# Two feed-forward layers whose output product is done in a second phase, as seven block products over eleven pairs

## The reference, cut to what matters

```python
def swiglu(x, w_in, w_out):
    gate, up = jnp.split(x @ w_in, 2, axis=-1)
    return (jax.nn.silu(gate) * up) @ w_out
...
        h = layer_norm(DEEPNORM_ALPHA * h + m, ln_mix_g[layer], ln_mix_b[layer])
        f = swiglu(h, ffn_w_in[layer], ffn_w_out[layer])
        h = layer_norm(DEEPNORM_ALPHA * h + f, ln_ffn_g[layer], ln_ffn_b[layer])
```

## Time and profile before

| what | value |
|---|---|
| median of three runs | 2750.70 us (2750.08 to 2753.43) |
| profiled execution, span from first to last instruction | 2747.0 us |
| the same execution's granted clock, mean share of full speed | 0.968 |
| matmuls of PE in it | 13124 |

### The profile page before, as it was taken

One profiled execution on the slowest core, in us unless ns is written; L12 is line 12 of the kernel. 1 busy time (PEld: TensorE's weight loads), 2 busy tenths in 40 slices (PEclk: granted clock), 3 DMA queues, 4 the chain that ended last, 5 costly groups with the idle time before them and its releaser, 6 DMA issues. The chain is left out here.

```text
span 2747.0 us, 40526 instructions
## 1 busy us (share of the span) xinstructions
PE 2554.0 (93%) x13124; PEld 2139.3 (78%) x13124; DVE 1835.2 (67%) x3179; ACT 818.5 (30%) x1382; POOL 830.4 (30%) x600
## 2 busy tenths in 40 slices
PE   6787699999999999978999999997899999999996
PEld 5676577878888888866888888886787888888885
DVE  8879527776666666583667666667577666666666
ACT  3223323332332232213222233222134223322321
POOL 2968320333332332411111111110024333323332
PEclk8889899999999999998999999998899999999998
DMA  4333214134443443412010110100404344434431
GB/s 138 91 100 108 81 39 153 43 105 140 126 122 107 133 119 108 145 54 69 24 39 23 38 31 23 38 23 16 153 28 119 110 140 125 122 107 134 118 117 75
DMA packets 388063, 246.16 MB, mean 90 GB/s; under 512 B 23936, under 2 KB 370176, under 8 KB 387072
## 3 DMA queue, kind: packets, MB, share of 16 engines
q1 hardware_dynamic: 387968, 244.92, 29.9%
HBM read 227.10 MB, written 17.76 MB: 89 GB/s over the span
## 5 line engine op out<-in xcount | busy, mean ns | idle before, releaser
L968 DVE TENSOR_TENSOR h<-h,ps 128x512 f32<-128x512 f32 x320 | 218.9, 685 | 154.8 <-PE ps L542 154.4
L2209 POOL TENSOR_TENSOR w_lo<-w_raw_plain,w_hi 128x1024 fp32r<-128x1024 f32 x38 | 91.8, 2423 | 556.2 <-ACT w_hi L62 556.2
L2237 PE MATMUL ps<-aT_hi,w_hi 128*128 128x512 f32 x624 | 251.6, 403 | 3.7 <-DVE hg_q_raw L2498 1.9
L2237 PE MATMUL ps<-aT_hi,w_lo 128*128 128x512 f32 x624 | 246.2, 394 | 0.0
L2237 PE MATMUL ps<-aT_lo,w_hi 128*128 128x512 f32 x624 | 244.7, 392 | 0.0
L1086 POOL TENSOR_TENSOR s5o_w_sets_plain<-s5o_w_sets_plain 128x512 f32<-128x512 f32 x100 | 138.0, 1385 | 220.4 <-DMA s5o_w_sets_plain<-in_ffn_w_in_dram 220.4
L1086 POOL TENSOR_TENSOR hgo_w_sets_plain<-hgo_w_sets_plain 128x512 f32<-128x512 f32 x100 | 137.2, 1376 | 221.6 <-DMA hgo_w_sets_plain<-in_ffn_w_in_dram 221.6
L484 PE MATMUL ps<-aT_hi,hgo_w_sets 128*128 128x512 f32 x640 | 203.1, 393 | 1.1 <-DVE hgo_w_sets L912 1.1
L484 PE MATMUL ps<-aT_hi,s5o_w_sets 128*128 128x512 f32 x640 | 203.0, 393 | 1.1 <-DVE s5o_w_sets L912 1.1
L542 PE MATMUL ps<-s5o_w_hi,s5o_hid_hi 128*128 128x512 f32 x352 | 138.2, 393 | 14.1 <-DVE aT_lo L905 13.5
L62 ACT ACTIVATE s5o_w_sets<-s5o_w_sets_plain 128x512 fp32r<-128x512 f32 x152 | 92.7, 627 | 177.3 <-POOL s5o_w_sets_plain L1086 151.2
(11 more groups left out here) (394 smaller groups left out, 6344.3 us busy)
## 6 DMA issues: line engine op xcount, KB each, us to landing
s5o_w_sets_plain<-in_ffn_w_in_dram SPq DMA_DIRECT2D x208, 256.0 KB, 3.3
hgo_w_sets_plain<-in_ffn_w_in_dram SPq DMA_DIRECT2D x208, 256.0 KB, 3.3
w_raw_plain<-in_hg_w_in_dram SPq DMA_DIRECT2D x40, 512.0 KB, 4.1
s5o_w_sets_plain<-in_ffn_w_in_dram SPq DMA_DIRECT2D x96, 128.0 KB, 2.6
hgo_w_sets_plain<-in_ffn_w_in_dram SPq DMA_DIRECT2D x96, 128.0 KB, 2.7
s5o_w_lo_plain<-in_ffn_w_out_dram SPq DMA_DIRECT2D x11, 1024.0 KB, 5.0
hgo_w_lo_plain<-in_ffn_w_out_dram SPq DMA_DIRECT2D x11, 1024.0 KB, 5.0
h<-in_x_dram SPq DMA_DIRECT2D x4, 1024.0 KB, 8.9
```

Source lines behind the costliest of these rows:

```text
L968: v.tensor_tensor(to, to, ps[:, 4 + m % 4, :], ALU.add).then_inc(S["out_acc"], 1)
L2209: g.tensor_tensor(w_lo[b][:, :, :], w_raw[b][:, :, :], w_hi[b][:, :, :].bitcast(F32), ALU.subtract).then_inc(E[f"w_lo_done{b}"], 1)
L2237: ins = t.matmul(ps[:, half, :], w[b][:, kk, :], x[:, kk, cols], start=(kk == 0 and q == 0), stop=(kk == KT - 1 and q == 2))
```

## The change: what it does

- The output product is taken out of the loop. The loop only makes hidden tiles, two per iteration, and its two tiles use banks 0 to 3 and 4 to 7 in turn (`4 * second + to`). PE goes from position 13 straight to position 0 of the next iteration.
- The hidden pair and four sums or differences of it (`hidden_sum`, four operations on POOL for each pair) are stored to a DRAM scratch, seven 128x512 blocks for each of the 11 pairs, by SP.
- A second phase of 7 x 11 = 77 steps follows (`out_step`): for each of the seven products `OUT_PRODUCTS`, eleven pairs are accumulated in four PSUM banks (the other four for the next product). A step is 4 token tiles x 3 = 12 matmuls. Its operands are one stored block and one or two blocks of w_out, loaded by `load_pair`; DVE subtracts where there are two (`pair_sum`), ACT makes hi (`pair_hi`, 1024 columns), DVE lo (`pair_lo`). Eleven places form a ring; a place is reloaded when the step that used it is done, and at most six loads run ahead of `pair_hi`.
- DVE adds a finished product to h once for each product (`accumulate(p)`), placed six steps into the next one. In the last product the first two pairs go as before and the last nine go tile by tile (`last_tile`). The first layer now also normalises tiles 0 to 5 by way of ACT and POOL (`rescale`, `add_bias`).
- The order of ACT's and DVE's instructions in a tile is new (`tile`; `ahead(n)` is the split of the set n positions behind the first of the tile, which may belong to the next iteration). `SLOTS` and `SLOT_AT` are as before.

Of the code, cut to its core:

```diff
         return ("11", 0, "21-11") if tt < PAIRS else ("22", 1, "12-22")
...
+    OUT_PRODUCTS = ["11*11", "S1*T1", "S2*T2", "S4*22", "S3*T3", "12*21", "22*T4"]
+    A_PART = [0, 3, 5, 6, 4, 1, 2]
+    B_PARTS = [((0, 0),), ((0, 0), (0, 1)), ((1, 1),), ((1, 1),), ((0, 1), (1, 1)), ((1, 0),), ((1, 0),)]
+    B_SUM = [False, True, True, False, True, False, True]
...
+    LAST_STEPS = STEPS - NG
...
+    plain_homes = [k.plain[f"{tag}_home{n}"] for n in range(4)]
...
+    RING = [("home", 3), ("block", 3), ("block", 4), ("slot", 0), ("slot", 1), ("slot", 2),
+            ("hi", 0), ("hi", 1), ("hi", 2), ("hi", 3), ("lo", 3)]
+    LAST_RING = RING[6:8] + RING[0:6] + [("home", 0), ("home", 1), ("home", 2)]
+    EARLY_RING = 3
...
+            def store_early(j, of):
+                s.dma_start(scratch_part(j, 0, 1), first_half(of)).then_inc(S["early_stored"], 16)
+            def store_late(j):
+                s.wait_ge(S["hidden_sum"], 4 * j + 4)
+                carry(s, j)
+                s.dma_start(scratch_part(j, 1, 2), late_hidden).then_inc(S["late_stored"], 16)
+                s.dma_start(scratch_part(j, 3, 4), plain_homes[1][:, :]).then_inc(S["late_stored"], 16)
             def load_rows(gamma, beta):
...
+                final = isinstance(i, int) and i == LAST - 1
+                for pos in range(SLOTS, 10):
+                    load_set(i, pos)
                 if not (isinstance(i, int) and i == 0):
-                    load_w2(i)
-                for pos in range(SLOTS, 2 * NP):
+                    store_late(i - 1)
+                for pos in range(10, 2 * NP):
                     load_set(i, pos)
-                if not (isinstance(i, int) and i == LAST - 1):
+                s.wait_ge(S["merged"], (2 * i + 1) * NMERGE)
+                carry(s, i)
+                store_early(i, early_hidden)
+                if not final:
                     for pos in range(SLOTS):
                         load_set(i + 1, pos)
...
+            def load_pair(n):
+                p, j = n // NG, n % NG
+                before = used_before(n)
+                if before is not None:
+                    s.wait_ge(S["step"], before + 1)
+                if n >= IN_SEMS:
+                    s.wait_ge(S["pair_hi"], n - IN_SEMS + 1)
+                (_, plain), sem = pair_of(n)[1], S[f"set_in{n % IN_SEMS}"]
+                s.dma_start(first_half(plain), scratch_part(j, A_PART[p], 1)).then_inc(sem, 16)
+                tiles = (2 * j + 1, 2 * j + 2) if j < LAST else (0, NF_LAST)
+                for m, (q, dh) in enumerate(B_PARTS[p]):
+                    to = plain if m == len(B_PARTS[p]) - 1 else pair_of(n)[1][0]
+                    s.dma_start(second_half(to), w_out_v[:, tiles[q], dh * HALF:(dh + 1) * HALF]).then_inc(sem, 16)
...
+            s.wait_ge(S["late_stored"], 32 * LAST)
+            s.wait_ge(S["plain_hi"], 2 * len(PLAIN_SETS))
+            for n in range(EARLY_RING):
+                load_pair(n)
+            s.wait_ge(S["part"], 16)
+            for n in range(EARLY_RING, LAST):
+                load_pair(n)
+            store_late(LAST)
+            s.wait_ge(S["late_stored"], 32 * NG)
+            for n in range(LAST, LAST_STEPS):
+                load_pair(n)
+            s.wait_ge(S["out_acc"], accs_before(5))
             for to, of in first_weights:
...
                         t.wait_ge(S["kept"], 3 * (f - 1) + r - 3)
                         if r > 4:
                             t.wait_ge(S["merged"], (f - 1) * NMERGE + r - 4)
-                    elif not (isinstance(f, int) and f == 1):
-                        t.wait_ge(S["merged"], (f - 2) * NMERGE + (6, 7, 9, 8)[r])
+                    elif not (isinstance(f, int) and f <= 2):
+                        t.wait_ge(S["merged"], (f - 3) * NMERGE + (6, 7, 9, 8)[r])
+                    elif f == 2:
+                        pass
                     elif r == 0:
...
-            def outputs(i, tiles, hidden):
...
-                    for q in range(FG):
-                        for n, (x, w) in enumerate(((hid_hi, w2_hi), (hid_hi, w2_lo), (hid_lo, w2_hi))):
-                            ins = t.matmul(ps[:, 4 + m % 4, :], x[:, q, tt * P:(tt + 1) * P],
-                                           w[:, q, dh * HALF:(dh + 1) * HALF],
...
+            def pair_product(n, tt):
+                p, j = n // NG, n % NG
+                (a_hi, a_lo), (b_hi, b_lo) = operands(n)
+                rows = slice(tt * P, (tt + 1) * P)
+                for m, (x, w) in enumerate(((a_hi, b_hi), (a_hi, b_lo), (a_lo, b_hi))):
+                    ins = t.matmul(ps[:, out_bank(p, tt), :], x[:, rows], w, start=(j == 0 and m == 0),
+                                   stop=(j == LAST and m == 2))
+                return ins
+            def out_step(n):
+                p, j = n // NG, n % NG
+                t.wait_ge(S["pair_lo"], n + 1)
+                if n == 0:
+                    t.wait_ge(S["merged"], (NF_LAST - 1) * NMERGE)
+                if n == NG:
+                    t.wait_ge(S["half_product"], 4)
+                if p >= 2 and j == 0:
+                    t.wait_ge(S["out_acc"], accs_before(p - 1))
+                if p == 2 and j == 0:
+                    t.wait_ge(S["first_copied"], PAIRS)
+                for tt in range(PAIRS):
+                    ins = pair_product(n, tt)
+                ins.then_inc(S["step"], 1)
+            def last_tile(tt):
+                for n in range(LAST_STEPS + EARLY_STEPS, STEPS):
+                    t.wait_ge(S["pair_lo"], n + 1)
+                    ins = pair_product(n, tt)
+                ins.then_inc(S["last_tile"], 1)
             for n, (dh, kh) in enumerate(PIECES):
...
-            def keep(f, n):
+            def keep(f, n, second):
                 a.wait_ge(S["product"], (f - 1) * NP + n + 1)
                 carry(a, f)
                 if n == 2:
                     a.wait_ge(S["merged"], (f - 1) * NMERGE + 4)
                     carry(a, f)
+                elif isinstance(f, int) and f == 1:
+                    a.wait_ge(S["half_product"], n + 1)
                 else:
-                    a.wait_ge(S["hid"], 2 * f)
+                    a.wait_ge(S["merged"], (f - 2) * NMERGE + (10 if n else 8))
                     carry(a, f)
-                a.activation(act_out[0 if n == 0 else 1][:, :], ps[:, n, :], ACT.Copy).then_inc(S["kept"], 1)
+                a.activation(act_out[0 if n == 0 else 1][:, :], ps[:, 4 * second + n, :], ACT.Copy).then_inc(S["kept"], 1)
...
+            def pair_hi(n):
+                p, j = n // NG, n % NG
+                (hi, _), (_, plain) = pair_of(n)
+                a.wait_ge(S[f"set_in{n % IN_SEMS}"], parts_in(n))
+                if B_SUM[p]:
+                    a.wait_ge(S["pair_sum"], sums_to(n))
+                    if p in (1, 2):
+                        a.activation(difference(j), second_half(plain), ACT.Copy)
+                split_hi(a, hi, plain).then_inc(S["pair_hi"], 1)
...
+            def tile(i, second):
+                f, final = 2 * i + 1 + second, isinstance(i, int) and i == LAST - 1
+                def ahead(n):
+                    pos = NP * second + n
+                    if pos < 2 * NP:
+                        set_hi(i, pos)
+                    elif not final:
+                        set_hi(i + 1, pos - 2 * NP)
+                ahead(4)
+                keep(f, 0, second)
+                ahead(5)
+                keep(f, 1, second)
+                ahead(6)
+                ahead(7)
+                keep(f, 2, second)
+                ahead(8)
+                silu_late(f)
+                ahead(9)
+                silu_early(f)
+                ahead(10)
...
+            def merge(f, step, second, to_hidden):
...
+                    10: (second_half(to_hidden), late, diff[:, :], ALU.mult)}[step]
                 v.tensor_tensor(to, one, other, op).then_inc(S["merged"], 1)
...
+            def pair_sum(n):
+                p, j = n // NG, n % NG
+                if B_SUM[p]:
+                    hi, lo = (second_half(a) for a in pair_of(n)[1])
+                    v.wait_ge(S[f"set_in{n % IN_SEMS}"], parts_in(n))
+                    if p == 2:
+                        v.wait_ge(S["pair_hi"], NG + j + 1)
+                    elif p == 6:
+                        v.wait_ge(S["pair_hi"], 2 * NG + j + 1)
+                    v.tensor_tensor(lo, lo, hi if len(B_PARTS[p]) == 2 else difference(j), ALU.subtract
+                                    ).then_inc(S["pair_sum"], 1)
+            def pair_lo(n):
+                v.wait_ge(S["pair_hi"], n + 1)
+                (hi, lo), (_, plain) = pair_of(n)
+                v.tensor_tensor(lo, plain, hi.bitcast(F32), ALU.subtract).then_inc(S["pair_lo"], 1)
...
+                ahead(4)
+                ahead(5)
+                merge_steps(1, 2)
+                ahead(6)
+                merge_steps(3, 4)
+                ahead(7)
+                merge_steps(5, 6)
+                ahead(8)
```

(25 more changed lines are left out.)

494 lines of the change are left out of this document (250 added, 244 removed).

## The result

The changed kernel takes **3023.05 us** in the median (3019.72 to 3025.55, 4 runs) where the kernel before takes 2750.56 (2750.08 to 2753.43): a ratio of 1.0984, 95% interval 1.0968 to 1.1001. Forecast were 2990 us, in a range from 2915 to 3060. The sign, the range and the mechanism are right; the forecast is 33 us short. One term, the clock, is short by 52 us over the 18 seams; other terms of the seam were too high and hide part of that. Of all executions behind the numbers of this document one was slow (6365.38 us at a granted clock of 0.421, in e12); it counts in no ratio, and only in that run's median.

A forecast was written before the change was run, and what follows sets the result against it. PE was taken to bound the kernel, busy 93% of the span and never stopping in the loop. Terms -60.2 + 293 + 12 - 5 = +240 on 2747.0 gave 2987 profiled, 2990 us median, range 2915 to 3060.

The forecast's parts named there:

- matmuls removed: Output product falls from 1056 to 924 matmuls a layer, at 0.228 us each: -60.2 us for both layers.
- seam, first wait: Passing between loop iterations, position 13 waits for ACT's third copy, behind the hi of next iteration's set 0: 7.3 us.
- seam, second wait: Next iteration's set 1 loads only after position 13; its 7.6 us chain, less 2.73 hidden by position 0: 4.9 us.
- seam, third wait: Position 6 waits for a third copy delayed by POOL's hidden sums among the sums for sets 5 to 7: 2.2 us.
- seam, clock: PE runs at half clock after the 7.3 us wait, nothing taken for the 4.9 us wait: 1.9 us a seam.
- into the second phase, both layers: Entering the second phase, first lo, plain sets 4 and 5 and first pair come late: +12 us, from 4 to 24.
- the 77 steps: Second-phase steps need 2.73 us of PE each, with ACT, DVE and loads keeping ahead: no extra time.
- last product and tail: First tile of the last product about 9 us late, against old waits gone and a shorter tail: together -5 us.
- Rival B: Only slot reuse holds, not ACT's order: position 0 starts 4.8 us late in each seam, 2784 us; chance 0.06.
- rival C: Clock falls at both waits of a seam and returns late, 4 us more a seam: 3062 us; chance 0.13.
- Rival D: Second phase bound by its loads at the loop's 130 GB/s, 100 us a layer: up to 3190 us; chance 0.05.
- What would show it: Predicted trace signs: loop PE busy some 70%, position 0 every 54.5 us, named waits, half clock once per seam.

The follow-up runs named there:

- e12: On e9, PE runs the third tile of the last product ahead of the transposes of tiles 0 and 1; 2712.0 us, ratio 0.9859.
- e4: Changed kernel with an extra lo x lo product in the second phase, 132 more matmuls in each layer; 3081.92 us, ratio 1.1191.
- e1: Changed kernel with ACT's third copy out of PSUM ahead of the hi of the set seven positions on; 2856.75 us, ratio 1.0388.
- e2: Changed kernel with only another slot table, each slot free at least four positions before its next use; 2728.85 us, ratio 0.9921.
- e10: On e5, a slot table in which position 0 of the next iteration reuses the slot of position 11; 2773.21 us, ratio 1.0079.
- e3: Changed kernel with the edits of e1 and e2 together, copy order and slot table; 2725.19 us, ratio 0.9906.
- e5: On e3, POOL makes the sum for set 5 first and the second pair of hidden sums behind the sum for set 6; 2718.54 us, ratio 0.9877.
- e6: On e3, SP loads plain sets 4 and 5 ahead of the store of the last pair's sums; 2722.01 us, ratio 0.9891.
- e8: On e3, the edits of e5 and e6 plus the sixth product's additions moved behind the last lo; 2715.9 us, ratio 0.9874.
- e9: On e8, first three pairs loaded ahead of norm rows and a store, five whole steps instead of two in the last product; 2709.51 us, ratio 0.9847.
- e11: On e5, second-phase steps that load one block of output weights load it twice, 768 KB in every step; 2730.67 us, ratio 0.9925.

## Why the prediction was right, and where it was not

| term | forecast, us | measured, us |
|---|---|---|
| matmuls removed | -60.2 | -57 to -59 (e4) |
| seam, first wait | 7.3 | 7.0 |
| seam, second wait | 4.9 | 4.7 |
| seam, third wait | 2.2 | 1.0 |
| seam, clock | 1.9 | 4.8 |
| seam, one of 18 | 16.3 | 17.5 |
| all seams | +293 | +315 |
| into the second phase, both layers | +12 | +20 |
| the 77 steps | 0 | 0 |
| last product and tail | -5 | about -3 |
| sum of the terms | +240 | +273 to +275 |
| in all | +240 | +277 in the profile, +272 in the medians |

What is left to +277 are 2.1 us ahead of the feed-forward part and the half clock at the start of the loop.

**Matmuls removed.** Right, and priced by themselves. 0.228 us is the price. By the 131 ns that the Trainium skill gives for a stream (TensorE: Matmul & The Clock Gate, back-to-back issue gap) e4's 264 matmuls would be an estimated 35 us; they cost 57 to 59.

**The seam's first two waits.** Right in place, engine and size to 0.3 us, each confirmed by taking it away: ACT's order is the first wait (e1), the table both (e2), and e10, with one more product in between, has 1.6 where the same rule gives 2.0. Rival B (slots only) described e1, not the change; its 4.8 us is what e1 has, but it left out the clock.

**The third wait.** Half the size, and the reasoning met the right engine by the wrong link. Forecast was the sum for set 7 with its hi ahead of the third copy; e1 and e3, where the copy goes first, still wait, and in e5, which moves the sums for sets 5 and 6 ahead, 2.2 of 8.2 us are left. The link is the lo of set 6 ahead of two merges. It probably came out at 1.0 because half clock at position 1 delays PE by some 2 us on its way to position 6; no run separates this.

**The clock** is the step that failed: "I take nothing for it" after the 4.9 us wait, with 1.9 for the seam. The clock falls behind both waits, and costs 4.8, so 2.9 us a seam were missing. That the seam still came out within 1.2 us of its forecast is in part luck, since the waits were taken 1.7 us too long together, the third most of all. This is rival C in its mechanism (a fall at both waits), though C took 5.9 us for the clock in all, 1.1 more than it cost. I drew a threshold between 3.47 us (no fall) and 7.04 (fall) and put 4.9 on the wrong side of it, on one row each. The Trainium skill (TensorE: Matmul & The Clock Gate, section on HAM oscillation) describes a fall in every pass of a loop that waits for its loads; the trace agrees, with two falls in each of the 18 passes.

**Into the second phase.** 20 where 12 was taken, inside 4 to 24. The waits are the forecast ones, 0.7, 0.6, 2.8 and 2.5 us, but half clock, 3 us in each layer, was again not in the sum. e6, e8 and e9 show how they hang together: the load behind the store, and then the first pair behind another store and the norm rows.

**The 77 steps** cost nothing, and e11 shows how far from binding the loads are. Rival D was priced too low: at 130 GB/s the 22 steps of 768 KB take 6.0 us each, not 4.0, so it would have been some 145 us a layer and not 100.

**Last product.** The wait for the first tile's lo's came, 6.0 us for a forecast 9, with 3.5 to 4 at half clock; the tail behind the last matmul is 14.9 us (before 17.0, forecast 12). Waits, half clock and tail together are 19.4 us where they were 21.0 in the first layer, and 25.0 for 26.1 in the second.

**What would show it.** Half clock once per seam: wrong, twice. PE busy at 70%: it is 83% of the window, since a matmul at half clock counts as busy for longer (0.63 to 0.79 us in place of 0.39); the count of matmuls, down from 445 to 325, would have been the right sign. The period of 54.5 us: 55.8 in the mean of nine (38.3 + 17.5). The others came as named, but for the one long wait a layer that stands under `issue`.

## What to carry to other kernels

Work in the cover of which something was loaded is not free to move: ask which slot each load waits for, and whether the distance from its last use to its next is longer than the chain from load to operand (here 7.5 us, three products). With a number of sets per pass that is no multiple of the slots (14 and 6), position mod slots leaves two slots with a distance of two; a table in which no distance is under four costs nothing and was worth 294 us. Where an engine's stream is carried out in order, look at what stands *behind* a late operation: two lines in exchange were worth 166 while the slots were late, and 3.7 once they were not. And count a wait of 4 us and more on PE with half clock behind it: in the feed-forward parts of these traces that held each time.
